# Second input projection and attention joined into one stage, eight projection tiles placed in pieces between the attention's steps, probabilities drained per head

## The reference, cut to what matters

```python
n = rms_norm_2(h, attn_norm_w)
proj = n @ w_in                       # 1024 x 2816: 22 tiles of 128 columns
aq, ak, av, rq, rk, rv, rg = split(proj)   # tiles 0-3, 4, 5, 6-9, 10-13, 14-17, 18-21
aq = rope(rms_norm_2(aq per head, q_norm_w)); ak = rope(rms_norm_2(ak per head, k_norm_w))
y_attn = windowed_gqa_sink(aq, ak, av, sink)   # 8 heads, 2 KV heads, query block b sees key blocks b-1, b, b+1
rq = rope(rq); rk = rope(rk) * HEAD_DIM ** -0.5
ret = bidirectional_retention(rq, rk, rv, ...) # then norm, gate with silu(rg)
h = h + concat([y_attn, y_ret]) @ w_out
```

## Time and profile before

| what | us |
|---|---|
| median of three runs | 2859.72 |
| the profiled execution's own time | 2863.25 |
| its span | 2861.2 |
| projection stage, in the span | 1496 to 1752 |
| attention stage | 1752 to 1891 |
| retention and what follows to the next stage | 1891 to about 2090 |

### The profile page before, as it was taken

One profiled execution on the slowest core, in us unless ns is written; L12 is line 12 of the kernel. 1 busy time (PEld: TensorE's weight loads), 2 busy tenths in 40 slices (PEclk: granted clock), 3 DMA queues, 4 the chain that ended last, 5 costly groups with the idle time before them and its releaser, 6 DMA issues. The chain is left out here.

```text
span 2861.2 us, 42833 instructions
## 1 busy us (share of the span) xinstructions
PE 2591.5 (91%) x18056; PEld 2011.7 (70%) x18056; DVE 1126.8 (39%) x1298; ACT 708.5 (25%) x1055; POOL 769.2 (27%) x440
## 2 busy tenths in 40 slices
PE   6984999999987999898979997668699999999999
PEld 5872777777766888543748885557577888887887
DVE  5335222222124222333363543753426766763000
ACT  3122222222221111112131102540134333332210
POOL 1223322122001222101242430001313655455621
PEclk8986999999988999999989998875599999999999
DMA  5126223323031111232322320000042222223431
GB/s 159 51 88 211 79 78 98 96 76 90 28 100 32 45 47 51 92 116 64 110 87 68 89 81 18 1 5 0 15 136 71 89 88 87 68 80 132 145 131 63
DMA packets 248723, 226.18 MB, mean 79 GB/s; under 512 B 34944, under 2 KB 213888, under 8 KB 248192
## 3 DMA queue, kind: packets, MB, share of 16 engines
q1 hardware_dynamic: 240656, 211.43, 23.9%
q10 hardware_dynamic: 7920, 12.59, 1.6%
HBM read 158.41 MB, written 57.70 MB: 76 GB/s over the span
## 5 line engine op out<-in xcount | busy, mean ns | idle before, releaser
L177 POOL TENSOR_TENSOR wlo<-wraw,whi 128x1024 fp32r<-128x1024 f32 x79 | 198.5, 2513 | 684.7 <-ACT whi L172 684.7
L2712 PE MATMUL tl_ps_bank<-tl_dn,tl_hid 128*128 128x512 f32 x1056 | 241.4, 391 | 2.5 <-POOL tl_dn L2418 2.5
L2712 PEld LDWEIGHTS tl_ps_bank<-tl_dn,tl_hid 128*128 128x128 f32 x1056 | 199.3, 189 | 44.4 <-issue 2.9
L977 PE MATMUL rs_ps_bank<-hT_hi,rs_f_hi 128*128 128x512 f32 x384 | 172.2, 448 | 32.8 <-POOL rs_f_lo L744 22.4
L1476 PE MATMUL mg_ps_proj<-y,mg_wb 128*128 128x512 f32 x384 | 167.6, 600 | 8.7 <-DMA mg_wb<-in_w_branch 8.7
L172 ACT CAST whi<-wraw 128x1024 fp32r<-128x1024 f32 x79 | 83.1, 1052 | 340.1 <-PE i_ps_ps L199 163.4
L2257 PE MATMUL tl_ps_bank<-tl_M,tl_ophi 128*128 128x512 f32 x528 | 167.0, 390 | 0.0
L199 PE MATMUL bc_ps_ps<-hT_hi,whi 128*128 128x512 f32 x384 | 151.7, 395 | 5.5 <-DVEq L1345 5.5
L977 PE MATMUL rs_ps_bank<-hT_lo,rs_f_hi 128*128 128x512 f32 x384 | 152.9, 398 | 0.0
L977 PE MATMUL rs_ps_bank<-hT_hi,rs_f_lo 128*128 128x512 f32 x384 | 152.7, 398 | 0.0
L199 PE MATMUL bc_ps_ps<-hT_lo,whi 128*128 128x512 f32 x384 | 150.2, 391 | 0.0
(11 more groups left out here) (409 smaller groups left out, 5290.2 us busy)
## 6 DMA issues: line engine op xcount, KB each, us to landing
wraw<-in_w_in SPq DMA_DIRECT2D x77, 512.0 KB, 4.0
scratch_pg<-rs_f_out SPq DMA_DIRECT2D x48, 256.0 KB, 2.3
mg_sg<-scratch_pg SPq DMA_DIRECT2D x24, 512.0 KB, 3.4
tl_raw<-in_w_gate SPq DMA_DIRECT2D x11, 1024.0 KB, 6.8
tl_raw<-in_w_up SPq DMA_DIRECT2D x11, 1024.0 KB, 5.3
scratch_hid<-tl_H SPq DMA_DIRECT2D x11, 1024.0 KB, 4.9
tl_hidraw<-scratch_hid SPq DMA_DIRECT2D x22, 512.0 KB, 3.3
tl_dnraw<-in_w_down SPq DMA_DIRECT2D x44, 256.0 KB, 2.6
```

Source lines behind the costliest of these rows:

```text
L177: self.nc.gpsimd.tensor_tensor(self.lo[s][:, :], self.raw[s][:, :], self.hi[s][:, :].bitcast(F32), ALU.subtract).then_inc(self.lo_ready, 1)
L977: ins = mm(F[:, h, :], a[:, c], b[:, k, cols[h]], start=k == 0 and u == 0, stop=k == KD - 1 and u == 2)
L2712: ins = nc.tensor.matmul(bank[b][:, :], hid[k][:, x, c], dn[n % 2][:, v, :], start=k == 0 and j == 0, stop=k == FF - 1 and j == 2)
```

## The change

One function, `phase_mix`, takes the place of both. Tiles 0 to 8 are projected as before. V is flipped before tile 8. K's row for the first KV head is doubled in place and the second's stands in `Q[:, 17]`, through three transfers on SP placed ahead of the weight load of tile 10. Then come 16 units of attention. In each, every head is three transposes (two at the edges), then a `piece`: six of the 48 matmuls of a projection tile. Two units make a tile, so tiles 9 to 16 are done in the 16 units, into two banks `fill_ps`. `pt_ps` is one bank now, so each head's transposes wait until ACT has copied the head before (`pt_ready`, four per unit). Tiles 17 to 21 follow undivided. `y` is kept in `Q[:, 0:4]` (the input `h2` is still in use by the projection) and split into `y.hi`, `y.lo` after the last product: four copies on ACT, four subtractions on DVE. The loops over tiles are written out.

```diff
 # SP, ahead of the load of tile 10
+                        sp.wait_ge(rotated, 5)
+                        for to in range(2):
+                            sp.dma_start(Q[to * HEAD:(to + 1) * HEAD, 17, :], Q[HEAD:P, KEY, :]).then_inc(doubled, 16)
+                        sp.wait_ge(doubled, 32)
+                        sp.dma_start(Q[HEAD:P, KEY, :], Q[0:HEAD, KEY, :]).then_inc(doubled, 16)
...
 # ACT
                 def exchange(t):
+                    if t:
                         act.wait_ge(rotated, nth(t))
...
+                def after(T):
+                    if T + 2 < N:
+                        w.split_hi(act, T + 2, T % 2, T // 2 + 1)
...
+                    if 7 <= T <= ROPED:
+                        act.wait_ge(copied, 2 * T + 4)
+                        exchange(T - 1)
...
+                def probabilities(n, x):
+                    k = len(window(n // 2))
+                    act.wait_ge(probs, 4 * n + x + 1)
+                    if n:
+                        act.wait_ge(out, n)
+                    nc.scalar.copy(PT[:, x * k:(x + 1) * k, :], pt_ps[:, 0:k * P].rearrange("p (k c) -> p k c", c=P)).then_inc(pt_ready, 1)
...
+                for n in range(UNITS):
+                    if n and n % 2 == 0:
+                        keep(n // 2 - 1)
+                    for x in range(3):
+                        probabilities(n, x)
+                    if n + 2 < UNITS:
+                        exps(n + 2, range(2))
+                    probabilities(n, 3)
+                    if n + 2 < UNITS:
+                        exps(n + 2, range(2, 4))
+                    if n % 2:
+                        after(tile_after(n))
+                keep(NB - 1)
...
+                for t in range(4):
+                    w.wait_product(act, N - 1, 1)
+                    nc.scalar.copy(y.hi[:, t, :], Q[:, t, :]).then_inc(y_hi, 1)
 # DVE
                 def rotate(t):
+                    dve.wait_ge(swapped, nth(t) * 64 + 64)
+                    nc.vector.tensor_tensor(Q[:, t, :], Q[:, t, :], cos[:, :], ALU.mult).then_inc(cosed, 1)
                     dve.wait_ge(turned, nth(t) + 1)
...
+                for n in range(2, UNITS + 3):
+                    if n >= 3 and (n - 3) % 2:
+                        empty(tile_after(n - 3))
+                    if n < UNITS:
+                        mask(n)
+                    if n < UNITS + 2:
+                        normalize(n - 2)
+                    if n < UNITS:
+                        maximum(n)
+                    if n >= 3 and (n - 3) % 2:
+                        T = tile_after(n - 3)
+                        dve.wait_ge(copied, 2 * T + 6)
+                        turned_rows(T)
...
 # PE
+                    for x in range(4):
+                        if 4 * n + x:
+                            pe.wait_ge(pt_ready, 4 * n + x)
+                        pe.wait_ge(normal, 4 * n + x + 1)
+                        for k in range(len(keys)):
+                            ins = nc.tensor.transpose(pt_ps[:, k * P:(k + 1) * P], s[n % 3][:, x, k * P:(k + 1) * P], d.ident[:, :])
+                        ins.then_inc(probs, 1)
+                        piece(FIRST + n // 2, 4 * g + x)
+                    if n + 3 < UNITS:
+                        scores(n + 3)
+                    pe.wait_ge(pt_ready, 4 * n + 4)
```

More of the change, by code:

```diff
@@ L1610, in phase_in2 @@
         small = sh.sb("small", [P, 2 * NB])
[L1611 to L1616, removed]
+        sums = [sh.sb(f"sums{u}", [P, 6, 4]) for u in range(3)]
@@ new lines, in phase_mix @@
+        pt_ps, y_ps = sh.ps("pt", [P, HALF]), sh.ps("y", [P, HALF])
+        fill_ps = [sh.ps(f"fill{h}", [P, HALF]) for h in range(2)]
+        ps = [fill_ps[0], fill_ps[1], pt_ps, y_ps]
+        stat_ps, back_ps = s_ps[:, 0, 0:2 * NB], [s_ps[:, 1 + h, :] for h in range(2)]
+        y4 = y_ps[:, :].rearrange("p (q c) -> p q c", q=4)
+        (copied, squared, summed, root, step, widened, back, normed, swapped, turned, cosed, rotated, tables) = (
+            sh.sem(n) for n in "copied squared summed root step widened back normed swapped turned cosed rotated tables".split())
@@ new lines, in _ @@
+                for T in range(FIRST - 1):
+                    after(T)
+                for n in range(2):
+                    act.wait_ge(flipped, n + 1)
+                    nc.scalar.copy(V[:, 4 * n:4 * n + 4, :], s_ps[:, n, :].rearrange("p (b c) -> p b c", b=4)).then_inc(v_ready, 1)
+                after(FIRST - 1)
+                for n in range(2):
+                    exps(n, range(4))
+                for n in range(UNITS):
[10 more added lines that the diff above has]
+                        after(tile_after(n))
@@ L1723, in _ @@
                         link(nc.vector.reciprocal(small[:, :], small[:, :]))
-                        spread(nc.vector.tensor_copy, wide[:, :], small[:, :]).then_inc(widened, 1)
-                    if T >= 3:
-                        link(nc.vector.tensor_tensor(x_cos[:, :], row(T - 3), cos[:, :], ALU.mult))
+                        spread(nc.vector.tensor_copy, wide, small[:, :]).then_inc(widened, 1)
+                    if 3 <= T < 8:
                         rotate(T - 3)
[L1729 to L1734, removed]
-                        rotate(T - 2)
@@ L1857, in _ @@
+                pe.wait_ge(normed, NORMED)
                 for n in range(2):
@@ L1876, in scores, with piece @@
                     ins.then_inc(scored, 1)
+                def piece(T, k):
+                    if k == 0:
+                        w.wait_split(pe, T)
+                        pe.wait_ge(copied, 2 * T + 4)
+                    u, c = w.slot(T % 2), slice(k * P, (k + 1) * P)
+                    for h in range(2):
+                        for n, (a, b) in enumerate(((w.hi[u], h2.hi), (w.lo[u], h2.hi), (w.hi[u], h2.lo))):
+                            ins = nc.tensor.matmul(fill_ps[h][:, :], a[:, c], b[:, k, half[h]], start=k == 0 and n == 0, stop=k == KD - 1 and n == 2)
+                        if k == KD - 1:
+                            ins.then_inc(w.product, 1)
@@ L1900, in _ @@
                     ins.then_inc(out, 1)
+                for T in range(LAST, N):
+                    w.multiply(pe, T, T % 2, ps, h2, free)
+        w.end(N)
 def phase_retention(nc, d, w, Q, y, following):
```

266 lines of the change are left out of this document (110 added, 156 removed).

## The result

| | before | after |
|---|---|---|
| median of four runs each, us | 2859.78 (2857.01 to 2861.24) | 2881.95 (2879.48 to 2884.15) |
| profiled span | 2861.2 | 2879.5 |
| projection and attention, first matmul to retention's first | 395.4 | 421.3 |
| retention, to the output projection | 183.5 | 180.5 |
| output projection | 107.5 | 107.9 |

The changed kernel is slower: ratio 1.0078, 95% interval 1.0061 to 1.0096, or 22.2 us by the medians. The forecast was 2889, 29 more. The joined stage alone is 25.9 us longer in the profile. Retention and the feed-forward stage, where the two kernels have the same instructions, are 3.0 and 3.8 us shorter. Over all the kernels run here, whatever their edit, the first took 180.4 to 186.1 us and the second 674.3 to 678.1. Whether that is scatter of single executions or belongs to each kernel is not shown.

The account below looks back on a forecast made before the run. Projection was taken as bound by PE, attention by a chain from engine to engine. Six terms sum to 310.5 us against 281.3, 29.2 more, so 2889 us; own range 2868 to 2908, with two in ten outside 2858 to 2910.

Parts of the forecast that it names:

- entry: From tile 8's end to the first transposes: DVE's emptying, rotation, masks and first normalization take 15.0 us, bounds 12 and 18.
- Term 2: Sixteen attention units without any other wait: cycle 11.35 us with three key blocks, 170.3 us in all, bounds 155 and 178.
- Term 3: After tiles 9 to 14, ACT's exchange waits for DVE's rotation, delaying PE's second head: 6 x 8.0 = 48.0 us.
- Term 4: PE's clock is low after seven long waits (the six and the entry), 2.2 us each: 15.4 us, bounds 0 and 39.
- undivided tiles: Five undivided projection tiles after the units, with 0.7 us for the last y's copy: 55.1 us, bounds 54 and 57.
- Term 6: The stage's end: ACT copies four rows, DVE subtracts four of 1.4 us, others idle: 6.7 us, bounds 5.5 and 9.
- A: Rival: ACT's waits are covered, terms 3 and 4 shrink to 0 and 2.2, giving 2828 us; chance 0.11.
- D: Rival: the projection pieces stretch each attention unit by as much as they save; no separate chance given.
- 22 and then 30 us apart: Sign in the joined stage: six PE waits of about 8 us before a transpose, at these alternating spacings.
- a moved retention: Sign against the forecast, in the stage behind: retention was put at 0 change, at most 2 us.

Follow-up runs that it names:

- the timed kernel: Against the changed kernel, SP issues the exchange after the rotation and the odd unit's first transposes, with nothing of it on ACT: 2825.95 us, ratio 0.9884.
- the first remedy: Against the changed kernel, six exchanges on ACT moved behind the even unit's last exponentials: 2839.12 us, ratio 0.9925.
- a second remedy: Against the changed kernel, the exchange moved to SP and made to wait also for the odd unit's first transposes: 2825.95 us, ratio 0.9884.
- The run with zeros: Against the changed kernel, PE multiplies thirty times by zeros in each of the six long waits: 2876.47 us over nine runs, ratio 1.0047.
- the two timed kernels: SP's exchange waiting for the odd unit's first transposes, with DVE's small addition (2825.95 us) or a one-operand reduction in its place (2826.83 us).
- the two late ones: ACT's exchange behind the even unit's last exponentials, with DVE's small addition (2839.12 us) or a one-operand reduction in its place (2830.68 us).
- the last experiment: Against the kernel with timed exchange, early scores and one-operand reduction, POOL's subtraction waits for the following even unit's last normalization: 2822.50 us, ratio 0.9870.

## Why the prediction was right, point by point

Slower was right, and so was its cause; the size was 7 us too large by the medians, of which 4.2 lie in the sum below and the rest outside the stage. Each term, from the end of tile 8 (1609.55 in the profile after):

| term | forecast | measured |
|---|---|---|
| 1 entry | 15.0 | 14.9 |
| 2 sixteen units without the long waits | 170.3 | 172.1 |
| 3 wait behind ACT, six times | 48.0 | 44.0 |
| 4 low clock behind the waits | 15.4 | 14.1 |
| 5 undivided tiles | 55.1 | 55.5 |
| 6 the end | 6.7 | 5.7 |
| sum | 310.5 | 306.3 |

**The mechanism** was seen as forecast: six waits, each ended by ACT's copy of one head, the four DMAs before it, the rotation before these. Taking it away gave 54.7 us in the units, where terms 3 and 4 without the entry's 2.0 measure 56.1; the timed kernel still lost 1.6 to a low clock in its first even unit. Of the rivals, A described what the timed kernel then did: without the waits the change pays. That its 2826 is so near the 2828 worked out is partly luck: its stage was 28.8 us shorter than before, not 32. D fell: the pieces are worth 44 to 50 us. One sign was given wrongly: the waits were to be 22 and then 30 us apart. They came 31.9 to 32.9 apart, which is what the sum's own pair of units with one wait makes (22.7 + 8.0 + 2.2).

**Term 3 was the mis-sized step.** It put the second head at 9.8 us behind the first. It came at 1657.49 - 1648.33 = 9.16, or 7.4 later than the usual 1.74, where I had 8.0. I took 3.0 us for the two steps of the rotation, from means of five (1.39 and 1.64). In each of them one instruction met POOL and took 2.05 and 3.31; the others took 1.22 to 1.25. Here they took 1.22 and 1.23. Four issues took 2.44, at the low bound.

**Term 2** hid a part that I had not seen. The even units without a wait took 11.3 us, as worked out (11.35), but odd ones 11.7, because of POOL beside the small addition: with the reduction in its place they took 11.2. In this kernel that is 0.4 us a pair; in the first remedy it was 1.9 in three even units, a held scaling in the other three, and the low clock. The forecast named POOL only for 128x1024 additions, never for one of four elements, and this is why rival A's number needed a second remedy.

**Term 4**: 12.1 us in six even units, 2.0 each, and 2.0 at the entry. The run with zeros bought back 10.7 of the 12.1. The estimate of 0.84 us a wait from the Trainium skill, page "TensorE: Matmul & The Clock Gate", section "HAM oscillation — how this bites in real kernels", was less than half of what the rows show. The cost of issuing, which the Trainium skill, page "DMA: Bandwidth & Descriptors", section "Issuing engines are not separate DMA queues", calls usually small beside the DMA, was a third of the wait (15.0 of 42.2 us, by the run in which SP issued).

**Term 6**: DVE's four subtractions took 4.63 us together, 1.16 each, not 1.4.

**The stages behind** were put at no change. By the profile they were 6.4 us shorter together, 3.0 of it in retention, and I had named a moved retention as a sign against me. In the experiments, whose code is the same from there on, retention took 180.4 to 186.1 us with no relation to their edits (180.4 and 182.3 in the two timed kernels, 183.7 and 180.5 in the two late ones), so the sign was badly chosen. What sets these levels stays open. It accounts for the gap between 25.9 in the stage and 22.2 by the medians only as far as single profiles can tell.

## What to carry to other kernels

When work is woven into a chain, list for each engine what now stands ahead of the instruction the busiest engine waits for, and give an in-order engine that serves it no wait on something late: here moving four DMAs and their wait from ACT to SP, at the right moment, turned 22 us lost into 34 gained. After such a repair read again the few tenths between the last producer and the next transposes: an instruction of four elements there can cost 2 us if another engine's long operation is let loose beside it. Replacing the instruction that is held may only pass the hold on to the next one; moving the long operation in time, as the last experiment does, took it away. And compare the changed stage in the profiles as well as the medians: stages behind it with the same code can differ by more than the edit is worth.

## What the runs showed of the hardware

- POOL's operations of 128x1024 held DVE's addition of 128x4 until they ended. In the kernels with the addition it met one of them 49 times, took 0.43 to 2.32 us, and ended 0.02 us after POOL each time; the other 79 times it took 0.15 or 0.16. A reduction of 128x8 in its place stayed at 0.15, and a scaling of 128x384 behind it was held instead (four took 2.82 us, not 1.41). DVE's mask, which reads PSUM and SBUF, took 1.74 to 1.76 us with and without POOL beside it.
- Four DMA issues in a row held ACT for 2.44 us in the changed kernel's units, and for up to 3.66 in the others; they held SP for 2.41 to 3.66.
- After PE idled 6.5 to 7.3 us, the next two heads took 1.5 to 2.5 us more in all. Behind waits of 2.9 us the clock fell some of the times and not others (in one kernel behind 2.89, and not behind 2.90). Zero products in the gap raised the mean clock of the units from 0.87 to 0.98 and gave 10.7 us back in the stage.
